# Two-layer encoder on one core: key transposes ahead of the second query projection, and the last expert's rows put in token order on the chip

## What is computed

```python
q = (h @ w_q).reshape(B, nC, CHUNK, B_KV_HEADS, B_GROUP, B_HEAD_DIM)
q = rms_norm(q, q_gain) * (B_HEAD_DIM ** -0.5)          # the second query projection and its norm
logits = jnp.einsum('bcqhgd,bcjhd->bchgqj', q, k_band) + band_bias
...
top_val, top_idx = lax.top_k(t @ w_router + b_router, 2)
wts = jax.nn.softmax(top_val, axis=-1)
y = swiglu(x_of_expert, w_in[e], w_out[e])              # for each expert e, over its tokens
out = jnp.zeros_like(t).at[buf_tok].add(y * buf_w[:, None])
x = x + g_f * out
```

## Time and profile before

| what | value |
|---|---|
| time, median of 3 runs | 1625.86 us (1618.68 to 1629.87) |
| the profiled execution: its own time, its span | 1620.67 us, 1618.3 us |
| PE busy, mean granted clock | 1483.9 us (92%), 0.955 |
| DVE busy | 1292.6 us (80%) |
| ACT busy | 988.1 us (61%) |
| POOL busy | 98.5 us (6%) |
| DMA moved | 501.40 MB, mean 310 GB/s |

### The profile page before, as it was taken

How to read it: one execution, slowest core, us unless ns; L and a number is a source line. 1 busy time by engine, 2 the same in 40 slices (tenths; PEclk the granted TensorE clock), 3 DMA queues, 4 the chain that set the end, 5 groups by cost and what they waited for, 6 DMA issues and landing times.

```text
span 1618.3 us, 22481 instructions
## 1 busy us (share of the span) xinstructions
PE 1483.9 (92%) x6600; PEld 1184.2 (73%) x6600; DVE 1292.6 (80%) x1396; ACT 988.1 (61%) x1284; POOL 98.5 (6%) x149
## 2 busy tenths in 40 slices
PE   6796879999976997899999999999999999999994
PEld 2584557777745666788888888888888888888883
DVE  5896649787664654898999989989899899899984
ACT  3355624344433732677778778778677777777772
POOL 3111111111010000000000000000000000000001
PEclk9797889999997798999999999999999999999997
DMA  9987139998554025799999999999999999999992
GB/s 339 396 318 271 58 126 326 313 345 302 194 221 169 1 88 212 272 378 362 395 384 366 393 379 371 396 377 371 393 376 373 394 374 373 381 375 375 390 373 93
DMA packets 216976, 501.40 MB, mean 310 GB/s; under 512 B 18449, under 2 KB 43233, under 8 KB 216929
## 3 DMA queue, kind: packets, MB, share of 16 engines
q1 hardware_dynamic: 192370, 425.04, 71.4%
q0 software_dynamic: 19760, 71.89, 12.1%
q10 hardware_dynamic: 4800, 3.90, 0.7%
HBM read 487.13 MB, written 13.63 MB: 309 GB/s over the span
## 4 chain that ended last, share of the span: by engine, by line
PE 84%; DVE 9%; DMA 4%; ACT 2%; issue 2%; POOL 0%; DVEq 0%; ACTq 0%; POOLq 0%
PE PS L1345 80%; DMA SHR<-in_ada_w 2%; DVE MOD L916 2%; PE PS L1691 2%; DVE WLO L904 1%; DVE HT_LO L957 1%; PE PS L1416 1%; DMA SHR<-toep_rows 1%; ACT WHI L576 1%; DVE ss L966 1%; DVE Q L975 0%; PE PS L1375 0%; DMA MOD<-in_ada_b 0%; DMA MOD<-y_rows,tok_row 0%; DVE sm L995 0%
## 5 line engine op out<-in xcount | busy, mean ns | idle before, releaser
L904 DVE TENSOR_TENSOR WLO<-WRAW,WHI 128x1024 fp32r<-128x1024 f32 x790 | 915.4, 1217 | 93.0 <-ACT WHI L576 92.9
L576 ACT ACTIVATE WHI<-WRAW 128x1024 fp32r<-128x1024 f32 x790 | 778.3, 1053 | 79.7 <-PE PS L1345 72.6
L1345 PE MATMUL PS<-WHI,HT_HI 128*128 128x512 f32 x1280 | 512.3, 400 | 30.9 <-DVE WLO L904 21.3
L1345 PE MATMUL PS<-WLO,HT_HI 128*128 128x512 f32 x1280 | 503.3, 393 | 0.0
L1345 PE MATMUL PS<-WHI,HT_LO 128*128 128x512 f32 x1280 | 430.4, 393 | 0.0
L1345 PEld LDWEIGHTS PS<-WHI,HT_HI 128*128 128x128 f32 x1280 | 243.6, 190 | 83.7 <-issue 18.9
L1345 PEld LDWEIGHTS PS<-WHI,HT_LO 128*128 128x128 f32 x1280 | 242.9, 190 | 52.3
L1345 PEld LDWEIGHTS PS<-WLO,HT_HI 128*128 128x128 f32 x1280 | 243.9, 191 | 48.5
L1345 PE MATMUL PS<-WHI,AT_HI 128*128 128x512 f32 x536 | 214.9, 401 | 6.0 <-DVE WLO L904 6.0
L1345 PE MATMUL PS<-WLO,AT_HI 128*128 128x512 f32 x536 | 209.9, 392 | 0.0
L1345 PE MATMUL PS<-WHI,AT_LO 128*128 128x512 f32 x536 | 209.8, 391 | 0.0
(11 more groups left out here) (185 smaller groups left out, 851.9 us busy)
## 6 DMA issues: line engine op xcount, KB each, us to landing
WRAW<-in_moe_w_in SPq DMA_DIRECT2D x448, 512.0 KB, 6.1
WRAW<-in_moe_w_out SPq DMA_DIRECT2D x224, 512.0 KB, 5.5
SHR<-in_ada_w POOLq DMA_DIRECT2D x80, 512.0 KB, 6.8
WRAW<-in_ffn_w_in SPq DMA_DIRECT2D x88, 256.0 KB, 6.8
WRAW<-in_a_w_qkv SPq DMA_DIRECT2D x24, 512.0 KB, 10.6
WRAW<-in_ffn_w_out SPq DMA_DIRECT2D x22, 512.0 KB, 4.8
SHR<-in_kv_ada_w POOLq DMA_DIRECT2D x16, 512.0 KB, 6.4
WRAW<-in_ada_w SPq DMA_DIRECT2D x16, 512.0 KB, 5.7
```

Source lines behind the costliest of these rows:

```text
L576: nc.scalar.activation(WHI[:, u.split(k), :], WRAW[:, u.raw(k), :], ACT.Copy).then_inc(w_hi, 1)
L904: V_.tensor_tensor(WLO[:, u.split(k), :], WRAW[:, u.raw(k), :], f32(WHI[:, u.split(k), :]), ALU.subtract).then_inc(w_lo, 1)
L1345: return nc.tensor.matmul(out, a, b, start=start, stop=stop)
```

## The change

**At the query projection.** PE transposes the shared keys before the projection and no longer after it. ACT splits units 0 and 1, scales the keys, and splits units 2 to 12 in one run; the squares of the norm come right behind. After the projection PE does 24 matmuls of 128x512 into bank 3 that nothing reads (`keep_clock`), then waits for the normed queries as before.

**In the expert loop.** Experts 0 to 6 still store their results, each in 128 rows of `y_rows`, which has one block per expert. The 8 stores that filled the second half of each expert's rows early in the program are gone. `rows` gives row 0 and weight 0 for a choice that is the last expert (or in the other pass). `selw` makes one more selection matrix per half of the tokens, for the last expert, with the token's weight in place of one. PE transposes both behind the first step of the last expert, and ACT copies them to `SELT`. POOL gathers the rows of experts 0 to 6 right after the store of expert 6, and DVE adds one of the four to `X` at the end of each of steps 2 to 5 of the last expert. The last expert's steps are written out on DVE.

**At the end.** ACT splits the last 4 units ahead of the copy of `AT_HI`. DVE makes `WLO` of the first two ahead of `AT_LO`, and of the other two behind it. `Y` is scaled in two halves; PE multiplies each with `SELT` for both halves of the tokens (4 float32 matmuls of 128x512), DVE adds the four results to `X`, and SP stores four quarters of the output as they come. The last expert's result is neither stored to nor gathered from `y_rows`.

The diff, cut to its core:

```diff
+        SELW = SHR[:, 2048:2304].rearrange("p (i s) -> p i s", i=TB)
+        SELT = SHR[:, 2304:2560]
...
+            def store(p):
+
+                for half in range(2):
+                    for i in range(TB):
+                        sp.wait_ge(out_ready, 2 * TB * p + TB * half + i + 1)
+                        cols = slice(half * 512, half * 512 + 512)
+                        sp.dma_start(out_v[:, i, cols], X[:, i, cols]).then_inc(out_stored, 16)
+                sp.wait_ge(out_stored, 32 * TB * (p + 1))
...
-            for b in range(TB):
-                sp.wait_ge(out_ready, b + 1)
-                sp.dma_start(out_v[:, b, :], PICKED[b][1]).then_inc(out_stored, 16)
-            sp.wait_ge(out_stored, 16 * TB)
...
-            pool.wait_ge(cst_landed, 16)
-            for e in range(N_EXP):
-                row = (e * TB + 1) * P
-                pool.dma_start(Y_ROWS.ap()[row:row + P, :].rearrange("p (r n) -> p r n", r=2),
-                               CST[:, 0:512].unsqueeze(1).broadcast_to([P, 2, 512])).then_inc(y_filled, 16)
...
-                for e in range(N_EXP):
+                for e in range(N_EXP - 1):
                     if e + 2 < N_EXP:
                         pool.wait_ge(g_psum, N_EXP * p + e + 2)
                         gathered(XG, H_ROWS, slot_tok[:, e + 2:e + 3], xg_landed)
                     pool.wait_ge(ey_ready, N_EXP * p + e + 2)
-                    row = (e * TB + p) * P
-                    pool.dma_start(Y_ROWS.ap()[row:row + P, :], Y).then_inc(y_stored, 16)
-                    pool.wait_ge(y_stored, 16 * (N_EXP * p + e + 1))
+                    if p and e == 0:
+                        for i in range(TB):
+                            pool.wait_ge(picked[i], 32)
+                    pool.dma_start(Y_ROWS.ap()[e * P:(e + 1) * P, :], Y).then_inc(y_stored, 16)
+                    pool.wait_ge(y_stored, 16 * ((N_EXP - 1) * p + e + 1))
+                pool.wait_ge(rows_ready, p + 1)
+                if p:
+                    pool.wait_ge(x_picked, 2 * TB)
+                for i in range(TB):
+                    for k in range(2):
+                        gathered(PICKED[i][k], Y_ROWS, tok_row[:, 2 * i + k:2 * i + k + 1], picked[i])
...
             u = Units(U_BQ)
-            hi(u, *range(0, 8))
+            hi(u, 0, 1)
             transposed(0, lambda n: KBT[:, 2 * n:2 * n + 2, :].rearrange("p j k -> p (j k)"), 4,
                        range(0, 2), kbt_psum)
-            hi(u, *range(8, 13))
+            hi(u, *range(2, 13))
...
+                step(Units(base + e * E_STEPS * E_UNITS), e * E_STEPS + 1)
+                step(Units(base + (e * E_STEPS + 1) * E_UNITS), e * E_STEPS + 2)
+                act.wait_ge(selt_psum, p + 1)
+                nc.scalar.activation(SELT, PS[:, 7, 0:TB * P], ACT.Copy).then_inc(selt_ready, 1)
+                with act.Fori(2, E_STEPS - 1) as j:
                     step(Units(base, e * E_STEPS + j, E_UNITS), j + (e * E_STEPS + 1))
+                hi(Units(base + (MOE_STEPS - 1) * E_UNITS), *range(0, 4))
                 at(MOE_STEPS - 1)
-                hi(Units(base + (MOE_STEPS - 1) * E_UNITS), *range(0, 4))
...
-                    first_row = iota[:, 0:N_EXP].unsqueeze(1).broadcast_to([P, TB, N_EXP])
-                    chain(V_.scalar_tensor_tensor(at3, first_row, float(TB * P), pos, ALU.mult, ALU.add))
+                    at, share, part, valid = pick[:, 0, :], pick[:, 1, :], pick[:, 2, :], pick[:, 3, :]
+                    at3, part3, valid3 = (v.rearrange("p (i e) -> p i e", i=TB) for v in (at, part, valid))
+                    expert = iota[:, 0:N_EXP].unsqueeze(1).broadcast_to([P, TB, N_EXP])
+                    chain(V_.tensor_scalar(valid, pos2, 0.0, None, ALU.is_ge))
+                    chain(V_.scalar_tensor_tensor(valid, pos2, float(P), valid, ALU.is_lt, ALU.mult))
+                    chain(V_.scalar_tensor_tensor(valid3, expert, float(N_EXP - 1), valid3, ALU.is_lt, ALU.mult))
+                    chain(V_.scalar_tensor_tensor(at3, expert, float(P), pos, ALU.mult, ALU.add))
+                    chain(V_.tensor_tensor(at, at, valid, ALU.mult))
+                    chain(V_.tensor_tensor(share, wt2, valid, ALU.mult))
                     for k in range(2):
-                        chain(V_.tensor_scalar(chosen, rank2, float(k), None, ALU.is_equal))
-                        chain(V_.tensor_tensor(part, chosen, at, ALU.mult))
+                        chain(V_.scalar_tensor_tensor(part, rank2, float(k), share, ALU.is_equal, ALU.mult))
+                        chain(V_.tensor_reduce(small[:, 12 + 2 * k:14 + 2 * k], part3, axis=AX, op=ALU.add))
+                        chain(V_.scalar_tensor_tensor(part, rank2, float(k), at, ALU.is_equal, ALU.mult))
...
+                def selw():
+                    e = N_EXP - 1
+                    for i in range(TB):
+                        V_.tensor_scalar(SELW[:, i, :], iota, pos[:, i, e:e + 1], wt[:, i, e:e + 1],
+                                         ALU.is_equal, ALU.mult).then_inc(selw_ready, 1)
+
+                def add_picked(n):
+                    i, k = n // 2, n % 2
+                    dve.wait_ge(picked[i], 32 * (p + 1))
+                    if p:
+                        dve.wait_ge(out_stored, 32 * TB)
+                    if k:
+                        dve.wait_ge(x_picked, 2 * TB * p + n)
+                    V_.scalar_tensor_tensor(X[:, i, :], PICKED[i][k], tok_w[:, 2 * i + k:2 * i + k + 1], X[:, i, :],
+                                            ALU.mult, ALU.add).then_inc(x_picked, 1)
...
-                if not p:
-                    rows()
+                rows()
+                selw()
                 steps(0)
                 turn_over(0)
                 with dve.Fori(1, N_EXP - 1) as e:
                     steps(e, e - 1)
                     turn_over(e)
                 e = N_EXP - 1
-                steps(e, e - 1)
+                turn = e * E_STEPS
+                step(Units(base + turn * E_UNITS), turn + 1, e - 1)
+                for j in range(1, E_STEPS - 1):
+                    step(Units(base + (turn + j) * E_UNITS), turn + j + 1)
+                    if j >= 2:
+                        add_picked(j - 2)
+                assert E_STEPS - 3 == 2 * TB
+                lo(Units(base + (MOE_STEPS - 1) * E_UNITS), 0, 1)
                 at_lo(MOE_STEPS - 1)
-                lo(Units(base + (MOE_STEPS - 1) * E_UNITS), *range(0, 4))
-                y(e, base + (MOE_STEPS - 1) * E_UNITS + E_OUT)
+                lo(Units(base + (MOE_STEPS - 1) * E_UNITS), 2, 3)
+
+                dve.wait_ge(w_used, base + (MOE_STEPS - 1) * E_UNITS + E_OUT)
+                dve.wait_ge(y_stored, 16 * (N_EXP - 1) * (p + 1))
+                dve.wait_ge(x_picked, 2 * TB * (p + 1))
+                for half in range(2):
+                    cols = slice(half * 512, half * 512 + 512)
+                    V_.tensor_tensor(Y[:, cols], PS[:, 3 + half, :], MOD[:, MOD1[5], cols], ALU.mult
+                                     ).then_inc((ey_half, ey_ready)[half], 1)
+                for half in range(2):
+                    cols = slice(half * 512, half * 512 + 512)
+                    for i in range(TB):
+                        dve.wait_ge(sc_psum, 2 * TB * p + TB * half + i + 1)
+                        V_.tensor_tensor(X[:, i, cols], X[:, i, cols], PS[:, SCATTER[i] + half, :], ALU.add
+                                         ).then_inc(out_ready, 1)
...
-            for i in range(TB):
-                dve.wait_ge(picked[i], 32)
-                chain(V_.scalar_tensor_tensor(PICKED[i][0], PICKED[i][0], tok_w[:, 2 * i:2 * i + 1], X[:, i, :],
-                                              ALU.mult, ALU.add))
-                V_.scalar_tensor_tensor(PICKED[i][1], PICKED[i][1], tok_w[:, 2 * i + 1:2 * i + 2], PICKED[i][0],
-                                        ALU.mult, ALU.add).then_inc(out_ready, 1)
...
+            def keep_clock(bank, count):
+
+                for _ in range(count):
+                    mm(PS[:, bank, :], HT_HI[:, 0, 0:P], HT_HI[:, 0:2, :].rearrange("p k s -> p (k s)"))
...
-            project(Units(U_BQ), 0, 4)
...
+            project(Units(U_BQ), 0, 4)
+            keep_clock(3, 24)
...
+                    if isinstance(e, int):
+                        pe.wait_ge(selw_ready, TB * (p + 1))
+                        for i in range(TB):
+                            last = nc.tensor.transpose(PS[:, 7, i * P:(i + 1) * P], SELW[:, i, :], ident)
+                        last.then_inc(selt_psum, 1)
...
+                pe.wait_ge(selt_ready, p + 1)
+                for half in range(2):
+                    pe.wait_ge((ey_half, ey_ready)[half], (p + 1, N_EXP * (p + 1) + 1)[half])
+                    cols = slice(half * 512, half * 512 + 512)
+                    for i in range(TB):
+                        mm(PS[:, SCATTER[i] + half, :], SELT[:, i * P:(i + 1) * P], Y[:, cols]).then_inc(sc_psum, 1)
```

30 lines of the change are left out of this document (13 added, 17 removed).

## The result

The changed kernel took 1611.45 us against 1625.86, a ratio of 0.9921 (95% interval 0.9902 to 0.9939); two of its fifteen executions, of 5,227 and 8,388 us, are left out of that ratio, and the median of the other thirteen is 1610.54. Run again (`after_again`) it took 1608.53 against 1628.68, 0.9878 (0.9857 to 0.9899). So the two pairs give 14.4 and 20.2 us, and their intervals do not overlap. The forecast was 1603.0. The sign and the range held; the size was too large, and the first ratio misses the 1% on which 0.79 of the chances stood, while the second reaches it.

What follows compares the result with a forecast made beforehand. PE was taken to bound the kernel, with 84% of the last-ending chain. Savings of 15.7, 5.6 and 0.5 less losses of 1.2 and 0.3 gave 20.3 us, from 1623.3 to 1603.0; range 1593 to 1613.

Steps and rivals of the forecast that it cites:

- the 1% on which 0.79 of the chances stood: Whole kernel: faster by over 1%, about 16 us, given a chance of 0.79; slower 0.03, the rest 0.18.
- The end, 15.7 us: Behind the last `AT_LO`: earlier product, float32 matmuls, four adds and quarter stores save 15.7 us (14 to 17).
- The base, 1623.3: Starting time for the sum: middle of four times of the kernel before, 1618.68 to 1629.87 us.
- The query projection, 5.6: At the query projection: the norm's squares start at 508.6 in place of 514.23, saving 5.6 us.
- The unread matmuls, 0.5: Behind the projection: query transposes at full clock in about half the runs, heads at half; saves 0.5 us.
- The upper end, 6: Top of the 0 to 6 us range for what the unread matmuls' hold on the clock could save.
- The first rival (17%): The clock holds through the first attention heads: 5.4 us more saved, 1597.6 us; chance 17%.
- its reading of the earlier transposes: Eight transposes from 226.70, clock half before and full in 228 to 230: read as a chance that transposes raise it.
- The expert loop's start, -1.2: Ahead of the expert loop: three more small operations and two selection matrices while PE idles lose 1.2 us (0.6 to 2).
- The last expert, -0.3 and no cost for the adds: In the last expert: two more PE transposes lose 0.3 us; four DVE adds fit into waits, leaving 0.27 us each.
- The second, third and fourth rival: DVE lacks room in last expert, 1609.7 us, 12%; projection gives nothing, 1609.1 us, 6%; DVE waits for first gather, slower, 3%.

Runs made afterwards that it cites:

- route_fit: The changed kernel with `all_branch`'s jumps, row numbers made earlier, unread matmuls through eight attention heads and two in each of three routing waits; 1586.36 us.
- one_pass: The changed kernel with the last expert's scaled result and selection matrix rounded to fp32r, one record per final matmul; 1605.82 us, ratio 0.9870.
- all_branch: The changed kernel with the jump over the second expert pass taken ahead of the ending on SP, DVE and PE; 1607.10 us, ratio 0.9879.
- second and third execution of before: The kernel before, unchanged, profiled twice more; 1628.24 and 1626.97 us, ratios 0.9998 and 0.9987.

## Why the prediction was wrong, by its steps

**The end, 15.7 us: the step that failed.** It gave 10.4 in the first pair of profiles, and 11.2 by the means of the table. Up to the product all held: the product began 1589.98 (forecast 1589.8) and was ready 6.56 us behind `AT_LO`'s start (forecast 6.51), since the first two units were split ahead. Two terms were mis-sized. The float32 matmul was priced at 0.55 to 0.66 by a group's busy time over its count and its mean. Those 56 records are halves: two unread float32 matmuls leave four of them, as in `route_fit`.

```profile
604.29 1.88 PE L1399 MATMUL PS<-MOD,CST 128*128 128x512 f32 x4
```

So the price was 0.6 to 0.7 of one matmul, and with 0.92 the last add ended 1.39 us late. `one_pass` took 1.45 off. And "before, 1615.17 to 1618.3 were 3.1 us, I take the same" was wrong, since code is now fetched there and none was before: 7.07 us, 3.94 more. `all_branch`, with the jumps ahead of the last work, takes back 4.6 against this profile and 4.3 against the mean of both.

**The base, 1623.3: the second that failed.** I took the middle of four times, two of each kind, and worked the sum out in a profile of the faster kind. Against before's later medians (1627.3 to 1629.1) the change is worth 16 to 21 us. The middle of four lay 4 to 6 us under them. The clock that I read there (heads 0 to 5 at half, the rest at full) is one draw of several, and one profile could not say so. Four times spread over 11 us could have.

**The query projection, 5.6.** Right: 6.15 (36.32 - 30.17). PE's first matmul came 0.4 us later (forecast 0.65), the splits of units 8 to 12 were ready, and the squares waited for nothing.

**The unread matmuls, 0.5.** The forecast for the clock was right in its main part: transposes at full clock, heads at half. The upper end, 6, was somewhat low: with the clock held all the way it is 7.2. But these 24 alone hold nothing beyond the transposes, and dropping them costs nothing that the medians show. The first rival (17%) did not happen. In its reading of the earlier transposes, the eight at 226.70 were not alone: eight more ran from 224.25, at half clock and behind 8.89 us of idle time, so it was sixteen transposes, and nothing else on PE, ahead of the rise.

**The expert loop's start, -1.2.** Right in what it counted: PE's wait is 6.47 and was 5.33, +1.14. Before:

```profile
655.27 0.80 PE L1345 MATMUL PS<-WHI,HT_HI 128*128 128x512 f32 x1 [5.33 <-DVE WLO L904]
```

**The last expert, -0.3 and no cost for the adds.** The adds are right: the wait left is 0.34 (forecast 0.27). The 0.3 for two more transposes doesn't show: the loop to `AT_LO` is 0.27 us shorter. The second, third and fourth rival did not happen; no gather was late.

By the means of the table, with the second and third execution of before for the two stretches in which the clock differs, the steps come to 6.2 us (projection), -0.5 (squares to first activation step, the longer wait of 1.1 in it), 0.4 (loop) and 11.2 (end): 17.3 us. Taken from 1628 that is 1610.7; measured were 1611.45 and 1608.53. The first stretch is left out: it is 1.3 us shorter in the changed kernel by the means, but over the fifteen profiles whose code there is the changed kernel's it varies from 474.1 to 479.8 us. So what the eight stores that went are worth, put at nothing in the prediction, isn't shown.

## What to carry to other kernels

Before a sum is taken from a profile, ask where in the spread of its kernel's times that execution lies, and profile it twice: here one draw of the clock was worth 7 us, where the whole change is worth 14 to 21. Price a matmul by the time from its start to its result, not by a group's busy time over its count, since one instruction can leave two records, as the float32 matmuls here do. And when the last piece of work is moved or shortened, look at what the engines still do behind it: a jump over a large piece of code belongs ahead of the last work.

## What was not expected of the hardware

The granted clock differs from one execution of the same program to the next, in what looks like a few patterns: two profiles of the changed kernel agree within 0.02 us from the squares to the first activation step, three of the kernel before have 55.77, 57.14 and 61.66 for the same attention. Which pattern comes stays open. Jumps taken at the very end cost some 4 us with the fetch of code. Unread matmuls in waits of 2 us held the clock at 0.96, for 4.8 us of gain by the stretch, although each wait was short; in and ahead of the heads, where PE shows as busy all the time at half clock, the same brought 7.2 us.
